# Final layer norm: outputs pre-filled with the bias, rows scaled by ScalarE and stored by accumulating transfers

## The reference, cut to what matters

```python
def _layer_norm(x, g, b):
    mu = jnp.mean(xf, -1, keepdims=True)
    var = jnp.mean(jnp.square(xf - mu), -1, keepdims=True)
    y = (xf - mu) * lax.rsqrt(var + LN_EPS) * g + b

x = _layer_norm(ALPHA * x + mix @ w_out, ln1_g, ln1_b)
x = _layer_norm(ALPHA * x + _moe(x, ...), ln2_g, ln2_b)    # this one
return x, c1, n1, m1, buf_new
```

## Time and profile before

| What | Value |
|---|---|
| Runs of the kernel before | 982.0, 984.67, 986.25 us |
| Profiled execution | 985.3 us, of which the trace spans 984.0 us |
| TensorE busy | 879.1 us (89% of the span) |
| VectorE busy | 599.9 us (61%) |
| ScalarE busy | 385.1 us (39%) |
| GpSimd busy | 89.5 us (9%) |
| Last matmul ends | about 942.5 us |

### The profile page before, as it was taken

The page is one execution under the profiler, slowest core; times in us unless marked ns, Lnnn a source line. Parts: engine busy times, 40 slices in busy tenths (PEclk is TensorE's granted clock), DMA queues, the critical chain, the costliest instruction groups (busy, mean ns, idle before and its releaser), DMA issues.

```text
span 984.0 us, 14558 instructions
## 1 busy us (share of the span) xinstructions
PE 879.1 (89%) x5981; PEld 793.0 (81%) x5981; DVE 599.9 (61%) x829; ACT 385.1 (39%) x401; POOL 89.5 (9%) x81
## 2 busy tenths in 40 slices
PE   6999999999999988999999899199799999999920
PEld 6999879788898987999999898177678888888810
DVE  3634553544557263132332355769999999999958
ACT  3432121221323313222222102456657777777600
POOL 3000000000000000101001011100111111110052
PEclk9989999999999989899999999589999999999975
DMA  9761170451606133123221911398899999999562
GB/s 278 236 236 44 54 240 18 142 169 55 226 31 185 63 103 120 36 72 112 87 81 49 352 82 50 96 354 311 321 345 422 403 423 416 410 410 393 219 225 91
DMA packets 79679, 195.78 MB, mean 199 GB/s; under 512 B 3905, under 2 KB 56857, under 8 KB 67336
## 3 DMA queue, kind: packets, MB, share of 16 engines
q1 hardware_dynamic: 72456, 169.40, 47.3%
q0 software_dynamic: 7168, 25.58, 7.0%
HBM read 167.65 MB, written 27.31 MB: 198 GB/s over the span
## 4 chain that ended last, share of the span: by engine, by line
PE 80%; DVE 12%; ACT 3%; DMA 3%; issue 2%; SPq 0%; POOL 0%; DVEq 0%; ACTq 0%; POOLq 0%
PE psum L428 23%; PE psum L430 23%; PE psum L429 22%; DVE split_lo L1376 2%; PE psum L1807 2%; PE psum L1826 2%; PE psum L1817 1%; PE psum L2038 1%; DVE onehot L1473 1%; PE psum L1855 1%; DVE last_lo L1376 1%; DMA xn<-in_x_prompt_dram 1%; ACT split_hi L404 1%; PE psum L1841 1%; PE psum L1976 1%
## 5 line engine op out<-in xcount | busy, mean ns | idle before, releaser
L428 PE MATMUL psum<-x_hi,split_lo 128*128 128x272 f32 x704 | 210.9, 300 | 4.5 <-ACT ht L808 4.5
L430 PE MATMUL psum<-x_hi,split_hi 128*128 128x272 f32 x704 | 203.8, 290 | 0.0
L429 PE MATMUL psum<-x_lo,split_hi 128*128 128x272 f32 x704 | 203.7, 289 | 0.0
L1376 DVE TENSOR_TENSOR split_lo<-raw,split_hi 128x2048 fp32r<-128x2048 f32 x72 | 163.1, 2285 | 13.0 <-ACT split_hi L934 11.5
L423 DVE TENSOR_TENSOR split_lo<-raw,split_hi 128x2048 fp32r<-128x2048 f32 x35 | 80.1, 2289 | 133.5 <-ACT split_hi L404 133.4
L934 ACT CAST split_hi<-raw 128x2048 fp32r<-128x2048 f32 x72 | 137.5, 1913 | 53.3 <-PE psum L430 53.3
L428 PEld LDWEIGHTS psum<-x_hi,split_lo 128*128 128x128 f32 x704 | 134.4, 191 | 8.8 <-ACT ht L808 5.5
L429 PEld LDWEIGHTS psum<-x_lo,split_hi 128*128 128x128 f32 x704 | 134.4, 191 | 1.5 <-issue 1.0
L430 PEld LDWEIGHTS psum<-x_hi,split_hi 128*128 128x128 f32 x704 | 134.2, 191 | 0.0
L428 PE MATMUL psum<-split_hi,xgl 128*128 128x512 f32 x192 | 77.2, 402 | 2.8 <-DVE xgl L1532 2.8
L429 PE MATMUL psum<-split_lo,xgh 128*128 128x512 f32 x192 | 75.5, 393 | 0.0
(11 more groups left out here) (371 smaller groups left out, 1752.0 us busy)
## 6 DMA issues: line engine op xcount, KB each, us to landing
raw<-in_w_e_gate_dram SPq DMA_DIRECT2D x32, 1024.0 KB, 8.1
raw<-in_w_e_up_dram SPq DMA_DIRECT2D x32, 1024.0 KB, 7.7
raw<-in_w_e_down_dram SPq DMA_DIRECT2D x32, 1024.0 KB, 7.4
raw<-in_w_in_dram SPq DMA_DIRECT2D x26, 1024.0 KB, 5.6
cb<-in_state_C_dram SPq DMA_DIRECT2D x8, 1024.0 KB, 8.1
out_dram<-cb SPq DMA_DIRECT2D x8, 1024.0 KB, 6.1
y_slots<-ys POOLq DMA_DIRECT2D x15, 512.0 KB, 8.3
y_slots<-x_hi POOLq DMA_DIRECT2D x2, 2048.0 KB, 12.6
```

Source lines behind the costliest of these rows:

```text
L428: nc.tensor.matmul(out, a_lo, b_hi, start=first, stop=False)
L429: nc.tensor.matmul(out, a_hi, b_lo, start=False, stop=False)
L430: return nc.tensor.matmul(out, a_hi, b_hi, start=False, stop=last)
L1376: v.tensor_tensor(lo, raw2[:, n % MOE_SLOTS, :], hi.bitcast(F32), ALU.subtract).then_inc(w_lo, 1)
```

## The change

Four things change together. First, after the state load of the second head (`h == 1`), SP issues five transfers that write `ln2_b` to every row of both outputs, from DRAM to DRAM. Second, the load of `ln2_b` into `lnb` goes. Third, VectorE no longer does the last instruction of each tile: `fin_ok` is raised by (x - mean) * gain, and ScalarE multiplies the tile by the reciprocal deviation. Fourth, the five stores of SP go; GpSimd waits for ScalarE and issues, between its small power instructions, a transfer that adds the tile to what stands in the output.

```diff
+            if h == 1:
+                for i in range(PT):
+                    sp.dma_start(y_prompt[0, i * P:(i + 1) * P, :], ln2_b[0].partition_broadcast(P)).then_inc(bias_out, 16)
+                sp.dma_start(y_sample.rearrange("b t d -> (b t) d"), ln2_b[0].partition_broadcast(NS)
+                             ).then_inc(bias_out, 16)
...
-        sp.dma_start(lnb[:], ln2_b[0].partition_broadcast(P)).then_inc(ln_in, 16)
...
-        for i in range(NT):
-            r = ROWS[i]
-            sp.wait_ge(fin_ok, i + 1)
-            dst = y_prompt[0, i * P:(i + 1) * P, :] if i < PT else y_sample.rearrange("b t d -> (b t) d")
-            sp.dma_start(dst, x1[0:r, i, :]).then_inc(outs, 16)
...
+        pl.wait_ge(bias_out, 16 * NT)
         for i in range(NT):
             r = ROWS[i]
             pl.wait_ge(v2_ok, i + 1)
             nc.gpsimd.tensor_tensor(hrs[0:r, i:i + 1], hve[0:r, i:i + 1], minus_half[0:r, 0:1],
                                     ALU.pow).then_inc(r2_ok, 1)
+            pl.wait_ge(n2_ok, i + 1)
+            dst = y_prompt[0, i * P:(i + 1) * P, :] if i < PT else y_sample.rearrange("b t d -> (b t) d")
+            pl.dma_start(dst, x1[0:r, i, :], accum_op=ALU.add).then_inc(outs, 16)
...
+        for i in range(NT):
+            r = ROWS[i]
+            ac.wait_ge(fin_ok, i + 1)
+            ac.wait_ge(r2_ok, i + 1)
+            nc.scalar.activation(x1[0:r, i, :], x1[0:r, i, :], ACT.Copy, scale=hrs[0:r, i:i + 1]).then_inc(n2_ok, 1)
...
-        ve_.wait_ge(ln_in, 64)
+        ve_.wait_ge(ln_in, 48)
...
         def normal(i):
             r = ROWS[i]
-            last = v.scalar_tensor_tensor(x1[0:r, i, :], x1[0:r, i, :], hmv[0:r, i, 0:1], lng[0:r, :], ALU.subtract,
-                                          ALU.mult)
+            v.scalar_tensor_tensor(x1[0:r, i, :], x1[0:r, i, :], hmv[0:r, i, 0:1], lng[0:r, :], ALU.subtract, ALU.mult
+                                   ).then_inc(fin_ok, 1)
             if i < NT - 1:
-                tail.mark(last)
-                last = combine(i + 1, 1)
-            step2(last)
-            ve_.wait_ge(r2_ok, i + 1)
-            v.scalar_tensor_tensor(x1[0:r, i, :], x1[0:r, i, :], hrs[0:r, i:i + 1], lnb[0:r, :], ALU.mult, ALU.add
-                                   ).then_inc(fin_ok, 1)
+                step2(combine(i + 1, 1))
```

More of the change, by code:

```diff
@@ L343, in build @@
     xal_ok, dve_tail = sem("xal_ok"), sem("dve_tail")
-    fin_ok, v2_ok, r2_ok = (sem(n) for n in ("fin_ok", "v2_ok", "r2_ok"))
+    fin_ok, v2_ok, r2_ok, n2_ok, bias_out = (sem(n) for n in ("fin_ok", "v2_ok", "r2_ok", "n2_ok", "bias_out"))
     def z_room(eng, j):
```

## The result

| | Before | After |
|---|---|---|
| Median of 7 runs | 984.67 us (981.17 to 986.25) | 978.04 us (976.21 to 982.64) |
| Ratio to before, 95% interval | | 0.9947 [0.9925, 0.9968] |
| Profiled execution: time, span | 985.3, 984.0 us | 980.01, 978.7 us |
| Last expert's copy (L1548, now L1555) starts | 942.48 | 940.63 |
| First combine of a second expert starts | 954.69 | 952.72 |

The two medians are 6.6 us apart, about twice the forecast, and 978.04 lies 1 us under the lower end of the range. By the ratio the kernel takes 984.67 x 0.9947 = 979.5 us, which is inside. All three intervals leave out 1: the change is faster, by about half a per cent.

A forecast was written before the change was run, and what follows sets the result against it. VectorE was taken to bound the last stretch. Last issue at 977.05 plus 3.5 landing plus 0.1 gives 980.65 instead of 984.0, 3.35 us less; from the median 984.67 that is 981.3 us, range 979.0 to 988.5.

The forecast's parts named there:

- The bound: Last norm: VectorE sets the end; its period falls from 5.34 to 4.13 us, the last epsilon from 978.88 to 974.07.
- The end's path: After the last tile's power: ScalarE starts 0.10 later, takes 1.04, GpSimd issues 0.10 later, at 977.05 us.
- the 0.1 behind the landing: End of the span: 0.1 us between the last transfer's landing and the end was expected to stay.
- Landing and the adding's price: Last adding transfer, 128 KB: 3.5 us to land, between 2.2 (plain store) and 4.1 (a whole load ahead of it).
- The rate: Adding transfers of the last norm: half of queue 0's 371 GB/s, 186 GB/s, so 2.8 us for 512 KB.
- The issue: GpSimd, between its powers: issuing each adding transfer takes 0.6 us and costs nothing.
- The slack given: GpSimd, per tile: an issue may last 1.37 us before it delays the next power.
- The fills: Second head: five early transfers, 2.23 MB, take 7.3 to 31 us in an idle DMA stretch and cost nothing.
- the condition: Fills: without the cover of the idle DMA stretch, TensorE would wait for the weight chunk, microsecond for microsecond.
- The 0.5%: Whole kernel: 0.34% faster, below the about 0.5% (4.9 us) that measurement can tell, so counted as the same, chance 0.75.

The follow-up runs named there:

- dve_scales: Changed kernel with VectorE multiplying by the reciprocal deviation again and no work on ScalarE; ratio to before 0.9985, stretch from first combine to end 27.97 us.
- act_extra: Changed kernel with one tiny one-element instruction on ScalarE ahead of its five scalings; one run, stretch from first combine to end 25.74 us.
- gpsimd_plain: Changed kernel without the fills, GpSimd storing plainly instead of adding, bias addition left out; ratio to before 0.9947, stretch from first combine to end 25.25 us.
- added_twice: Changed kernel with a second adding transfer of each tile, into scratch rows, ahead of the one to the output; ratio to before 1.0042.
- fills_only: Kernel before with only the five early fills added, and a wait for them ahead of SyncE's stores; ratio to before 0.9996.
- fills_late: Changed kernel with the five fills moved from the second head to ahead of the experts' weight loads; ratio to before 1.0006.

## Why the prediction was right

**The bound.** It read VectorE as the bound of the last stretch and counted 1.2 us back for each of four tiles. The period fell from 5.34 to 4.14 (4.13 predicted), and the last tile's epsilon stands 19.41 us behind the first combine, predicted 974.07 - 954.69 = 19.38. dve_scales shows the coupling directly.

The mechanism, then, was as predicted; on the last tile's path several terms were off.

**The end's path.** The total is right to 0.02 us by luck: errors on both sides cancel. The last transfer is issued 22.99 us after the first combine (975.71 - 952.72), predicted 977.05 - 954.69 = 22.36. The 0.63 are: ScalarE's instruction 1.15, not 1.04 (0.11; the upper bound given), its start 0.37 after the power, not 0.10 (0.27; act_extra takes this away), GpSimd's start 0.30 after ScalarE, not 0.10 (0.20), and 0.05 up to the power's end. The 0.10 had been taken from a hand-over to VectorE; GpSimd's fetches already stood in the timeline before with 0.30 of idle "issue" ahead of each, and that row was the one to use:

```profile
951.23 0.94 POOL L704 DMA_INDIRECT ybk<-y_slots,dest_i  x1 [0.30 <-issue]
```

Against it the landing took 3.0, not 3.5, and the 0.1 behind the landing is not seen. Stretch predicted 980.65 - 954.69 = 25.96, measured 25.98.

**Landing and the adding's price.** The bounds were 2.2 and 4.1. The lower is exactly GpSimd's plain store (gpsimd_plain), and adding makes it 0.8 longer, not a whole load of 1.9. That the 0.8 are the read of the destination is the prediction's argument; no run parts it from the rest of an adding transfer. The value taken, nearer the upper end, was on the wrong side of the middle.

**The rate.** Half of queue 0's rate was taken, 186 GB/s; it is 205 (added_twice), against 400 to 420 for plain stores. That agrees with the rule of the Trainium skill, "Collectives: The Full Stack", "The bandwidth ceiling: the fold count and why AG ≠ RS ≠ AR", which states for collectives that a second read through the same ring halves the rate; whether that is the cause here no run shows. What the prediction did not see is that a large adding transfer takes 5.5 to land, so that they do overlap; it had expected each to land before the next is issued. It cost nothing, since the large one ahead of the last had stopped moving data half a microsecond before the last one's began.

**The issue.** 0.6 was taken, 0.82 to 0.99 is listed, and some 0.6 is what it holds GpSimd for. The slack given, 1.37, covers either. The rule of the Trainium skill in "SBUF — State Buffer", "SBUF: two separate sides", did not show as a delay: every issue but the last ran with VectorE busy, and they took 0.88 to 0.99 against the last one's 0.82. The plain issues differ likewise, 0.57 to 0.63 against 0.54, and the last tile is also the smallest, so the two are not parted. It was no test of the rule either. The page speaks of VectorE's 2-port modes, which the prediction left out, and no row tells the mode of the stats beside these issues.

**The fills.** Cost nothing was right (fills_only, and the equal stretches between SyncE's stores), and the condition was, too: they hide by where they stand (fills_late, 5.8 us). The bounds for their length were 7.3 and 31 us. The chunk load behind them was issued at 205.75 and took 15.0, landing at 220.75 when ScalarE needs it at 254.42. In the kernel before the same load was issued at 201.19 and took 10.5, landing at 211.7; the prediction's 206.7 was 5 us too early. So the fills put it back by 9.1 us, near the lower bound. SyncE spent 4.4 us on their five issues, not 2.3, which is inside its idle time as well.

**The 0.5%.** The measured ratios, 0.9947, 0.996 and 0.9954, all give a little more than the 0.34% of the forecast, and their intervals reach from 0.17% to 0.75%. The stretch gives 3.3 us, 0.34%. Over all 31 runs the changed kernel's mean is 980.1 and over the 92 runs of before 984.2, 4.1 apart with a standard error of 0.54 (from standard deviations of 2.7 and 2.3 us), so 95% goes from 3.0 to 5.2 us and holds the 3.3. Whether the remaining 0.8 us are chance is not settled, but no mark in the traces shows a part of the change that makes them: the stretch of the fills is equal to 0.01 us, and from the first store of rows to the last expert's copy, where the bias load is gone, the changed kernel's three traces have 369.56, 369.17 and 369.11 us against 369.26 before. The first series' 6.6 us between the medians did not come again (3.9 and 4.8 us in the other two), so a part of it was chance.

## What to carry to other kernels

Where one engine's stream sets the end, an instruction moved off it counts once per tile, but the last tile pays the whole path of the new route by itself: here 4.8 us came back and 1.5 were lost on the way ScalarE, GpSimd, adding transfer. Keep the old short route for the last tile alone and both are had (24.5 in place of 26.0 us). A constant term can be written to the output in an idle stretch and added to by the store; look for the stretch first, as the same fills in a busy one cost more than the change gives. Compare such kernels by a stretch between two marks in the trace, since here the work ahead of it moved by up to 6 us from trace to trace.

## What the runs showed of the hardware

- Adding transfers from SBUF to DRAM, rows of 4 KB: 205 GB/s in steady flow (added_twice), where plain stores reach 403 to 423; 512 KB lands in 5.5 us instead of 2.9, 128 KB in 3.0 instead of 2.2, both from GpSimd's queue.
- Its issue is listed with 0.82 to 1.00 us instead of 0.54 to 0.63, but the next instruction of GpSimd started 0.55 to 0.68 after its start (added_twice).
- GpSimd starts a transfer 0.28 to 0.31 us after what it waited for, SyncE 0.02 to 0.03. A power of GpSimd, or an instruction of VectorE or ScalarE behind a power, starts 0.09 to 0.15 after it, but ScalarE's fifth scaling 0.37 to 0.38, cause open.
- Five transfers from one 4 KB row in DRAM to 2.23 MB of DRAM put back the landing of the chunk load behind them by 9.1 us: it was issued 4.6 later, and took 15.0 us to land instead of 10.5.
- The same multiplication of 128x1024 float32 by a number per row takes 1.15 us on ScalarE and 0.75 on VectorE; with the bias added from a second tile it takes VectorE 1.28.
